# Expert weights asked for eight chunks ahead, the two experts of a pair multiplied one behind the other, and softplus sums in two rounded parts

## What is computed

```python
for e in range(N_EXPERTS):                      # 32 experts
    hid = jax.nn.silu(t @ w_eg[e]) * (t @ w_eu[e])   # w_eg, w_eu: 1024 x 512
    out = out + gates[:, e:e + 1] * (hid @ w_ed[e])  # w_ed: 512 x 1024
```

```python
sp = jnp.where(valid, jax.nn.softplus(z), 0.0)
later = lax.cumsum(sp, axis=3, reverse=True) - sp
a = jnp.where(valid, jnp.exp(jax.nn.log_sigmoid(z) - later), 0.0)
```

## Time and profile before

| | us |
|---|---|
| median of 3 runs | 1775.36 |
| lowest, highest | 1773.78, 1776.03 |
| the profiled execution | 1774.61 |
| its span in the trace | 1772.8 |
| TensorE matmul busy in it | 1685.0 (95%) |
| VectorE, ScalarE, GpSimd busy | 894.3, 752.4, 111.8 |
| rate of the DMAs over the span | 232 GB/s |

### The profile page before, as it was taken

The page is one execution under the profiler, slowest core; times in us unless marked ns, Lnnn a source line. Parts: engine busy times, 40 slices in busy tenths (PEclk is TensorE's granted clock), DMA queues, the critical chain, the costliest instruction groups (busy, mean ns, idle before and its releaser), DMA issues.

```text
span 1772.8 us, 25754 instructions
## 1 busy us (share of the span) xinstructions
PE 1685.0 (95%) x10708; PEld 1308.8 (74%) x10708; DVE 894.3 (50%) x1502; ACT 752.4 (42%) x1154; POOL 111.8 (6%) x117
## 2 busy tenths in 40 slices
PE   7998989889998989999999999999999999999998
PEld 6976334433443369888899988888888889988886
DVE  6584211121112065644478977536654457987743
ACT  4563011111111145645556455424665545645532
POOL 0000000000000001400200000000240110000000
PEclk9998999999999999999999999999999999999999
DMA  7444999999999946323333454535423333354552
GB/s 285 164 155 190 421 427 429 428 429 428 427 430 428 425 181 238 125 114 143 143 143 143 170 207 186 204 145 230 192 103 143 143 143 144 143 190 184 188 206 84
DMA packets 31813, 412.15 MB, mean 232 GB/s; under 512 B 3648, under 2 KB 5216, under 8 KB 6496
## 3 DMA queue, kind: packets, MB, share of 16 engines
q1 hardware_dynamic: 31712, 410.70, 58.0%
HBM read 408.85 MB, written 1.84 MB: 232 GB/s over the span
## 4 chain that ended last, share of the span: by engine, by line
PE 83%; DMA 9%; DVE 3%; ACT 2%; issue 1%; SPq 0%; POOL 0%; POOLq 0%; DVEq 0%; ACTq 0%
PE bank L1145 9%; PE bank L1294 8%; PE bank L1299 8%; PE bank L1295 8%; DMA work_mem<-in_w 7%; PE bank L1713 7%; PE bank L1330 4%; PE bank L1329 4%; PE bank L1328 4%; PE bank L1717 3%; PE bank L1168 3%; DMA wring<-in_w 2%; PE bank L1354 2%; PE bank L1355 2%; PE bank L1360 2%
## 5 line engine op out<-in xcount | busy, mean ns | idle before, releaser
L1997 ACT ACTIVATE w_hi<-wring 128x2048 fp32r<-128x2048 f32 x84 | 161.1, 1918 | 222.8 <-PE bank L1329 101.3
L2763 DVE TENSOR_TENSOR w_lo<-wring,w_hi 128x2048 fp32r<-128x2048 f32 x84 | 192.2, 2292 | 121.7 <-ACT w_hi L1997 121.7
L1997 ACT ACTIVATE w_hi_early<-wring 128x2048 fp32r<-128x2048 f32 x84 | 160.7, 1914 | 201.3 <-PE bank L1295 136.7
L1294 PE MATMUL bank<-mixed,w_hi_early 128*128 128x256 f32 x928 | 232.3, 288 | 3.5 <-DVE w_lo L2763 3.5
L1295 PE MATMUL bank<-mixed,w_hi_early 128*128 128x256 f32 x928 | 227.3, 283 | 0.0
L2763 DVE TENSOR_TENSOR w_lo<-wring,w_hi_early 128x2048 fp32r<-128x2048 f32 x84 | 191.7, 2286 | 44.5 <-ACT w_hi_early L1997 44.1
L1294 PEld LDWEIGHTS bank<-mixed,w_hi_early 128*128 128x128 f32 x928 | 177.5, 191 | 8.4 <-DVE w_lo L2763 4.1
L1145 PE MATMUL bank<-wring,gates_mem 128*64 128x512 f32 x768 | 171.7, 604 | 11.4 <-DMA wring<-in_w 11.4
L1295 PEld LDWEIGHTS bank<-mixed,w_hi_early 128*128 128x128 f32 x928 | 177.8, 192 | 0.1
L2665 DVE TENSOR_TENSOR gates_mem<-bank,gates_mem 128x512 f32<-128x512 f32 x32 | 22.1, 692 | 251.0 <-ACT gates_mem L1945 140.6
L1145 PEld LDWEIGHTS bank<-wring,gates_mem 128*64 128x64 f32 x768 | 57.8, 139 | 113.2 <-issue 113.1
(11 more groups left out here) (504 smaller groups left out, 3072.7 us busy)
## 6 DMA issues: line engine op xcount, KB each, us to landing
wring<-in_w SPq DMA_DIRECT2D x160, 2048.0 KB, 8.6
work_mem<-in_w SPq DMA_DIRECT2D x32, 2048.0 KB, 18.1
cst<-in_const SPq DMA_DIRECT2D x1, 1224.0 KB, 15.9
prm<-in_prm SPq DMA_DIRECT2D x3, 381.0 KB, 7.9
x_mem<-in_x SPq DMA_DIRECT2D x2, 512.0 KB, 4.5
out_x<-x_mem SPq DMA_DIRECT2D x2, 512.0 KB, 2.6
rel_skew<-work_mem SPq DMA_DIRECT2D x1, 768.0 KB, 3.5
work_mem<-in_prm SPq DMA_DIRECT2D x1, 512.0 KB, 16.7
```

What stands on the lines that cost most here:

```text
L1294: pe.matmul(out, w[0][:, k, cols], x[0][:, k, :], start=(k == 0), stop=False)
L1997: act.activation(hi, w, ACT.Copy).then_inc(hi_ready, 1)
L2763: dve.tensor_tensor(lo, w, hi, ALU.subtract).then_inc(lo_ready, 1)
```

## The change

It has six parts.

1. **Eight chunks ahead.** Chunks 0 and 2 are asked for at the two early places, with chunk 6 and the second half of chunk 3 right behind (3.5 chunks); at `pre["out"][3]` come chunks 1, the first half of 3, 4 and 5; when both `member` tiles are there, chunk 7 in two halves. Chunks 6 and 7 of turn 0 have places of their own (`ahead_six`, `ahead_seven`), the slots of all others are turned by eight. Chunks 8, 10 and 12 wait for the first expert's half of the gate and up jobs of turn 0 (`first_half_used`) and chunks 9, 11 and 13 for the whole job. From chunk 14 on the waits are those of before. The row of gains for the last norm is asked for behind the last expert chunk, not in front of the block's end.
2. **One expert behind the other.** `hidden` and `down` take the expert outside and the slices inside, in all turns; each expert's chunk has its own wait. `down_half` of the last turn stays as it is.
3. **Routing.** `member` comes straight out of the positions of the two best experts; the weights (`gate_values`) are worked out behind `one_hot`, for both tiles at once. The second `h2_copy` goes from VectorE to ScalarE. The low part of the second tile is made in two halves, one ahead of the rank's sum and one behind `one_hot`.
4. **Ranks.** `strict` and `one` are copied once to rounded operands, and the rank matmuls are one record each.
5. **Softplus.** GpSimd splits the softplus values of a pair of heads into a rounded high part and a rounded rest, two instructions over 128 x 768, and TensorE's `again` multiplies both parts in single-record matmuls; it waits for GpSimd (`pool_step`) in place of VectorE.
6. Some tiles lie elsewhere in `work_mem`, so that chunk 6 has room.

```diff
-        for c, j in ((2, pre["vd"][1]), (4, pre["pv"][1]), (0, pre["out"][3]), (1, pre["out"][3]), (3, pre["out"][3]),
-                     (5, pre["out"][3])):
...
+        ahead_chunk(0, pre["vd"][1])
+        ahead_chunk(2, pre["pv"][1])
+        sp.dma_start(ahead_six, expert_source(6, 0)).then_inc(x_loaded[0], 16)
+        cols = slice(CHUNK_COLS // 2, CHUNK_COLS)
+        sp.dma_start(ahead_slot(3)[:, cols], expert_source(3, 0)[:, cols]).then_inc(x_loaded[0], 16)
+        ahead_chunk(1, pre["out"][3])
+        ahead_chunk(3, pre["out"][3], slice(0, CHUNK_COLS // 2))
+        ahead_chunk(4, pre["out"][3])
+        ahead_chunk(5, pre["out"][3])
+        sp.wait_ge(member_ready, TT)
+        for n, half in enumerate(ahead_seven):
...
+        for g in range(AHEAD_CHUNKS, AHEAD_CHUNKS + MOE_SLOTS):
+            c = g - AHEAD_CHUNKS
+            j = chunk_user(moe, c)
+            if c % 2:
+                sp.wait_ge(bank_full[j.bank], j.count(0))
+            else:
+                sp.wait_ge(first_half_used, 16 + c // 2 + 1)
+            expert_chunk(g % turn_chunks, g // turn_chunks)
...
-                w = [weight(name, pair, e).rearrange("p (k n) -> p k n", k=KT) for e in range(2)]
-                for k in range(KT):
...
-                    for e in range(2):
...
+                for e in range(2):
+                    half, w = slice(e * CAP, (e + 1) * CAP), hidden_weight(name, pair, e)
+                    for k in range(KT):
...
+                        mm = pe.matmul(psum[j.bank][half, :], x_e[:, k, pair, half], w[k], start=(k == 0), stop=(k == KT - 1))
+                    if e == 0 and r is first_pass and isinstance(turn, int) and turn == 0:
+                        mm.then_inc(first_half_used, 1)
...
-                    pe.matmul(b[:, 0:384], C("sufneg"), sp_, start=False, stop=False, skip_group_check=True)
-                    pe.matmul(b[:, P:S], negtriu[:, P:S], sp_[:, S:384], start=False, stop=False, skip_group_check=True)
+                    b, minus = psum[j.bank], sufneg_r[:, 0:1].to_broadcast([P, P])
+                    for part in (sp_hi, sp_lo):
+                        pe.matmul(b[:, 0:384], sufneg_r, part[:, n + r, :], start=False, stop=False, skip_group_check=True)
+                    for part in (sp_hi, sp_lo):
+                        pe.matmul(b[:, P:S], minus, part[:, n + r, S:384], start=False, stop=False, skip_group_check=True)
...
-                        pe.wait_ge(sb_ready, 8 * l + n + 2)
+                        pe.wait_ge(pool_step, 1 + 8 * l + n + 2)
...
+            for n in range(0, SB_N, 2):
...
+                pool.wait_ge(sb_ready, 8 * l + n + 2)
+                pool.tensor_copy(flat(sp_hi[:, two, :]), flat(p_s[:, two, :])).then_inc(pool_step, 1)
+                pool.wait_ge(pool_step, 1 + 8 * l + n + 1)
+                pool.tensor_tensor(flat(sp_lo[:, two, :]), flat(p_s[:, two, :]), flat(sp_hi[:, two, :]),
+                                   ALU.subtract).then_inc(pool_step, 1)
...
-            dve.wait_ge(r_exp, i + 1)
-            dve.wait_ge(top_exp, i + 1)
...
+            then(dve.tensor_scalar(pick1[:, i, :], iota8, idx_f[:, i, 1:2], None, ALU.is_equal))
+            then(dve.scalar_tensor_tensor(picked[:, i, :], iota8, idx_f[:, i, 0:1], pick1[:, i, :], ALU.is_equal, ALU.add))
+            dve.tensor_tensor(in_groups(member, i), every_group(picked, i), by_group(i), ALU.mult).then_inc(member_ready, 1)
```

More of the change, by code:

```diff
@@ L495, in program @@
     yT_all, mixed = view(yt_mem, 0, 16, S), view(xn_mem, 0, KT, S)
+    sp_hi, sp_lo = (view(parts(f"sp_{n}", "work_mem", first, 8 * 384), 0, 8, 384) for n, first in (("hi", 9216), ("lo", 6144)))
+    sufneg_r = parts("sufneg_r", "gates_mem", 5376 + 384 + 256, P)[:, :]
     w_lo = parts("w_lo", "wring", 0, RING * CHUNK_COLS)
@@ L704, in _, with ahead_chunk @@
+        def ahead_chunk(c, j, cols=slice(0, CHUNK_COLS)):
             sp.wait_ge(bank_full[j.bank], j.count())
[L705 to L715, removed]
+            sp.dma_start(ahead_slot(c)[:, cols], expert_source(c, 0)[:, cols]).then_inc(
+                first_pass.w_landed[(c + AHEAD_CHUNKS) % MOE_SLOTS], 16)
@@ L1104, in weight, with hidden_weight @@
                 c = MOE_CHUNKS.index((name, pair, n))
-                pe.wait_ge(r.w_landed[c % MOE_SLOTS], moe_landed(c, at))
+                if r is more_passes:
+                    pe.wait_ge(r.w_landed[c % MOE_SLOTS], moe_landed(c, at))
+                else:
+                    pe.wait_ge(r.w_landed[c % MOE_SLOTS], first_landed(c, at))
                 return moe_slot(c)
+            def hidden_weight(name, pair, n):
+                c = MOE_CHUNKS.index((name, pair, n))
+                if r is first_pass and isinstance(turn, int) and turn == 0:
+                    if c < MOE_SLOTS:
+                        pe.wait_ge(r.w_landed[(c + AHEAD_CHUNKS) % MOE_SLOTS], 16)
+                        if c == 3:
+                            pe.wait_ge(x_loaded[0], 48)
+                        slots = [ahead_slot(c)]
+                    elif c == MOE_SLOTS:
+                        pe.wait_ge(x_loaded[0], 48)
+                        slots = [ahead_six]
+                    else:
+                        pe.wait_ge(x_loaded[1], 48)
+                        slots = ahead_seven
+                else:
+                    slots = [weight(name, pair, n)]
+                tiles = KT // len(slots)
+                return [v[:, k * 512:(k + 1) * 512] for v in slots for k in range(tiles)]
             def pick():
@@ L1112, in pick @@
                     ready(j)
+                    if r is first_pass and isinstance(turn, int) and turn == 0 and n % 2 == 0:
+                        pe.wait_ge(xn_lo_ready, 2 + n // 2)
                     for k in range(2):
```

130 lines of the change are left out of this document (85 added, 45 removed).

## The result

The changed kernel takes 1876.3 us (1872.2 to 1876.8, four runs), the kernel before 1775.7 us beside it (1773.8 to 1776.1): ratio 1.0563, 95% interval 1.0549 to 1.0578. It is slower by 100 us where 11.5 us less was forecast. Rival A of the prediction came true: TensorE looks four records ahead, not 16.

A forecast was written before the change was run, and what follows sets the result against it. The DMA weight stream was taken to bound the expert stage, TensorE the stick-breaking stretches. Stage -7.1 (-9.8 - 1.9 + 4.6), expert order 0 and softplus -4.4 gave -11.5 us: 1764 us, range 1757 to 1774.

The forecast's parts named there:

- Rival A: Expert stage: TensorE sees fewer than eight records past a blocked one; about 1844 us at four, chance 0.15.
- the 5.3 us of the prediction: Expert stage: TensorE's spare time per turn, its 53.57 us against the weight stream's 58.9 us.
- My answer to it: Attention scores and L1463 records: the trace shows TensorE passing over at least four waiting records of one array half.
- The far end of rival A: Expert stage: no passing over of waiting records at all, a turn of 88 us and about 1995 us.
- Part 1, the first gate job earlier: Routing before the expert stage: shorter chain and rank matmuls start the first gate job earlier, -1.9 us.
- Part 1, the stream: Expert stage: two more chunks in ahead bring -9.8 us, late slots in turns 0 and 1 cost +4.6 us.
- the wait of 3.04 us for a chunk: Turn 0: TensorE's idle time taken as waiting for a chunk, subtracted from 56.61 us to give 53.57 us.
- rival B: Turns 0 and 1: second expert lags, each turn 4 us longer, extra chunks' gain lost; 1771 us, chance 0.11.
- Part 5: Stick-breaking in the hybrid layers: softplus split saves 0.28 us for each of 16 heads, -4.4 us, GpSimd's work hidden.
- The head at 0.71 us: Stick-breaking: TensorE's time for one head with the split softplus, 0.71 us in place of 0.99.

The follow-up runs named there:

- e10_padded: e5_fall_through with 15 more waits at the end of TensorE's arm that is not run, moving later instructions; 1763.3 us, ratio 0.9925.
- e2_order_alone: The kernel before with only the loops of hidden and down turned, expert outside and slices inside; 1882.6 us, ratio 1.0603.
- e11_probe: The kernel before with groups of matmuls on the lower, then upper array half added behind TensorE's last; one execution, upper half started 6 ns behind record 13.
- e1_side_by_side: The changed kernel with the loops of hidden and down as before, slices outside and experts inside; 1769.5 us, ratio 0.9963.
- e5_fall_through: e1_side_by_side with the two arms of TensorE's branch on crowded exchanged, the run arm right behind the branch; 1765.9 us, ratio 0.9948.
- e3_blocks_of_4: The kernel before with hidden changing experts after every four slices (eight records), down as before; 1783.7 us, ratio 1.0039.
- e6_before_fall_through: The kernel before with only the two arms of TensorE's branch on crowded exchanged; 1775.0 us, ratio 0.9999.

## Why the prediction was wrong, point by point

- **What bounds the kernel:** right, as far as it went. Before, the stream does. TensorE had little to spare, though more than the 5.3 us of the prediction: with neither wait nor branch in its way it does turn 0 in 51.7 us (`e10_padded`), so 7.1 us under a turn of 58.8 from the stream.
- **The step that failed:** in part 2, "At the loop's end the sequencer branched ... 18 records wait in the queue. 16 is within 18, just. I take it that the halves run side by side as before, and cost this part at 0." show how many records can wait, and I read it as how many TensorE looks through. These are two sizes: 18 wait, four are looked at. The earlier trace rows had shown a record starting beside the one four places ahead of it, three waiting records passed over and no more, and exactly that it is; rival A, held at 0.15, should have weighed far more. With a reach of four a turn takes 71.3 us in place of 58.7, over the stream's pace, and part 2 costs some 107 us (1882.6 in `e2_order_alone`, 1776.0 before beside it) where it was put at 0. The four that the trace showed were a measurement, the 16 an extrapolation by a factor of four.
- **The page's rule:** that matmuls start in program order (the Trainium skill, TensorE: Matmul & The Clock Gate, Part 3, What overlaps and what doesn't) is contradicted by `e11_probe` for the two halves of the array, within four records. My answer to it was right in kind, and then I took the whole queue for granted.
- **Rival A's price:** 67.4 us a turn at m = 4, measured 71.3. The mechanism was right, the term left out the ends of the three runs of jobs in a turn, where four records run alone: 3 x 4 x 0.43 = 5.2 us. Against that its base of 53.6 us was 1.9 too long, as above: 51.7 + 13.8 + 5.2 = 70.7. Hence 1844 forecast for it and 1876 measured. The far end of rival A, a turn of 88 us, adds up to about 2006 us and not 1995 by the prediction's own sum.
- **Part 1, the first gate job earlier:** forecast -1.9, measured -1.3 in this pair of executions, and -1.0 in the mean (168.66 over six kernels with the old routing, 167.70 over seven with the new), which scatter by about 1 us each. The chain itself is shorter by 1.8: from VectorE's row at 155.47 to the first gather at 162.41 before, 155.03 to 160.19 now. But the gather's records stay 0.21 us apart until 165.7 us in both kernels, and 0.12 after that. The granted clock is 0.50 from 156 to 165.7 us in both, the lower level, behind a stretch in which TensorE idled for the routing. So the earlier start falls into slow time, and the gather takes some 0.9 us longer.
- **Part 1, the stream:** the two chunks and the stalls were put at -9.8 and +4.6. In `e10_padded` the last chunk lands 6.8 us earlier behind the gate job and the layers start 5.9 us earlier, so -5.2 was about right once the order and the branch are out of the way; there the stream stalls for 0.3 us ahead of chunk 14 and 2.7 ahead of chunk 18, which leaves 6.8 of the 9.8. In the change as made nothing of it is left. The step that failed was the subtraction of "the wait of 3.04 us for a chunk" from turn 0: it was also the branch's wait, and grew to 4.06, and the slow down job behind it stayed. In `e1_side_by_side` the stream stalls for 5.4 us ahead of chunk 14 and 3.0 ahead of chunk 18 (forecast 1.1 and 3.5), and rival B's outcome, turn 0 eats the gain, came by another cause than B's.
- **Part 5:** -4.4 forecast, -3.1 measured. The head at 0.71 us was right (0.69). What was put at nothing, GpSimd's work beside VectorE, goes with the 1.6 us given back, at least where TensorE waits for the low part: through VectorE and not through a wait for GpSimd. The two instructions take 6.6 us and not 3.5, within the factor of two that I had allowed.
- **The sum:** with the old order of matmuls and a branch that falls through, the rest of the change gives 1763.3 us where 1764 was forecast, for a kernel which the change is not. Its profiled execution starts the gate job 0.9 us earlier, needs 5.9 us less from there to the layers and 3.1 less in them: 9.9 us, the difference of the spans, 1772.8 and 1762.9. The forecast had 1.9, 5.2 and 4.4.

`e10_padded` is faster than both kernels and computes all that they do: 0.9925 of before. Its lead over `e5_fall_through` seems to hang on where the code happens to lie, so an edit of TensorE's program in front of that point may undo it.

## What to carry to other kernels

Matmuls on different halves of the array run side by side here only as far as they stand within four records of each other in the program: alternate them, in blocks of four records at most, and end a run of them alternating. TensorE's busy share does not show the loss; the count of records in a stretch, or the length of one job, does. And where an engine idles at a branch, look at the sequencer's own rows before believing the releaser that the profile names: the arm that is usually run belongs right behind the branch, and the exit jump where the engine waits anyway.

## What the runs showed of the hardware

- A matmul record starts on a free half of the array once the record four places ahead of it has started, 6 ns later, for float32 and bf16, 512 and 128 columns. Up to 18 records wait in the queue at the same time.
- The jump of TensorE's sequencer over a whole arm took 3.9 to 7.1 us in the twelve kernels that have one. The branch that was not taken took 0.09 us, and the jump back at the end of the turns' loop 0.21 to 0.27 us, so a taken branch does not cost that by itself. In one kernel instructions came 3.9 us late a second time behind a jump, and did not when 15 more waits lay in front.
- Behind 2.1 to 4.1 us of idle time in turn 0 TensorE's granted clock was at its lower level for a while, and the next job of 16 records took 5.0 to 5.4 us in place of 3.65 (the kernel before, `e1_side_by_side`, `e3_blocks_of_4`, `e6_before_fall_through`).
- VectorE's subtraction of 128 x 2048 took 2.76 to 2.91 us where it started while an instruction of GpSimd ran, 2.28 where it started before it: longer by what GpSimd still had to run, less 0.14 us, eight times of eight.
